# Sparse attention with one query head per period, index dots between projection slices, x reloaded by tile

## The reference

```python
rel = relu(einsum("bqhd,bsd->bqhs", iq_b, ik))      # 8 index heads of 64, one normalised index key
score = einsum("bqh,bqhs->bqs", iw_b, rel)          # weighted sum over the index heads
score = where(causal, score, -inf)
_, idx = top_k(score, 128)                          # the 128 best keys of each query
logits = q . k[idx] * 128**-0.5                     # 8 query heads of 128, 2 key/value heads
o = softmax(logits, where valid) . v[idx]
mixed = sigmoid(gate_a + ..) * o_gdn + sigmoid(gate_b + ..) * o_dsa
h = x + mixed @ w_out
```

## Time and profile before

| | us |
|---|---|
| median of 3 runs (lowest, highest) | 2372.18 (2370.74, 2373.13) |
| the profiled execution's own time | 2367.97 |
| its span, first to last instruction | 2366.2 |
| PE busy | 2260.6 |
| DVE busy | 1294.7 |
| ACT busy | 918.6 |
| POOL busy | 464.0 |

### The profile page before, as it was taken

The page is one execution under the profiler, slowest core; times in us unless marked ns, Lnnn a source line. Parts: engine busy times, 40 slices in busy tenths (PEclk is TensorE's granted clock), DMA queues, the critical chain, the costliest instruction groups (busy, mean ns, idle before and its releaser), DMA issues.

```text
span 2366.2 us, 27907 instructions
## 1 busy us (share of the span) xinstructions
PE 2260.6 (96%) x10568; PEld 1825.0 (77%) x10568; DVE 1294.7 (55%) x2044; ACT 918.6 (39%) x1626; POOL 464.0 (20%) x387
## 2 busy tenths in 40 slices
PE   5999999898899999999998999999999989999997
PEld 4887888586678888877776788888777768888885
DVE  6768333395658486765665444433566654434343
ACT  4677343226532222243454322322445553222222
POOL 0000420030111010031454210101234542101012
PEclk9999999799999999999999999999999999999998
DMA  4231312121133333222111333333221113333322
GB/s 152 89 108 62 90 45 64 53 73 44 39 106 97 98 98 97 91 89 89 54 54 36 96 97 98 98 98 96 91 86 54 41 36 98 98 98 91 98 95 83
DMA packets 68901, 194.03 MB, mean 82 GB/s; under 512 B 14496, under 2 KB 18848, under 8 KB 68768
## 3 DMA queue, kind: packets, MB, share of 16 engines
q1 hardware_dynamic: 67584, 189.89, 26.1%
q10 hardware_dynamic: 1184, 2.36, 0.3%
HBM read 185.40 MB, written 6.82 MB: 81 GB/s over the span
## 4 chain that ended last, share of the span: by engine, by line
PE 82%; DVE 5%; ACT 5%; issue 4%; POOL 2%; DMA 1%; DVEq 1%; SPq 0%; POOLq 0%; ACTq 0%
PE bank L285 17%; PE bank L287 17%; PE bank L286 17%; PE bank L321 5%; PE bank L323 5%; PE bank L322 5%; PE bank L1616 3%; PE bank L965 1%; ACT b_wh L246 1%; PE bank L1153 1%; DVE b_wl L250 1%; PE bank L1644 1%; PE bank L1643 1%; PE bank L1008 1%; PE bank L1779 1%
## 5 line engine op out<-in xcount | busy, mean ns | idle before, releaser
L246 ACT ACTIVATE b_wh<-b_raw 128x1024 fp32r<-128x1024 f32 (+1 forms) x348 | 360.1, 1035 | 1089.3 <-PE bank L287 924.9
L250 DVE TENSOR_TENSOR b_wl<-b_raw,b_wh 128x1024 fp32r<-128x1024 f32 (+1 forms) x338 | 411.5, 1217 | 132.1 <-ACT b_wh L246 131.6
L285 PE MATMUL bank<-b_xh,b_wh 128*128 128x512 f32 x1216 | 477.5, 393 | 0.4 <-DVE b_wl L250 0.4
L286 PE MATMUL bank<-b_xl,b_wh 128*128 128x512 f32 x1216 | 474.6, 390 | 0.0
L287 PE MATMUL bank<-b_xh,b_wl 128*128 128x512 f32 x1216 | 474.5, 390 | 0.0
L285 PE MATMUL bank<-b_yh,b_wh 128*128 128x512 f32 x736 | 289.8, 394 | 14.8 <-POOL b_yl L573 7.0
L287 PE MATMUL bank<-b_yh,b_wl 128*128 128x512 f32 x736 | 287.2, 390 | 0.0
L286 PE MATMUL bank<-b_yl,b_wh 128*128 128x512 f32 x736 | 287.2, 390 | 0.0
L573 POOL TENSOR_TENSOR b_yl<-b_arena,b_yh 128x512 fp32r<-128x512 f32 x66 | 111.4, 1689 | 877.7 <-ACT b_yh L551 877.7
L321 PE MATMUL bank<-b_xh,b_wh 128*128 128x512 f32 x624 | 267.9, 429 | 14.0 <-ACT b_maskSb L1941 12.9
L285 PEld LDWEIGHTS bank<-b_xh,b_wh 128*128 128x128 f32 x1216 | 229.3, 189 | 51.8 <-issue 2.5
(11 more groups left out here) (373 smaller groups left out, 2967.1 us busy)
## 6 DMA issues: line engine op xcount, KB each, us to landing
b_raw<-in_zga SPq DMA_DIRECT2D x16, 512.0 KB, 3.7
b_raw<-in_c0up SPq DMA_DIRECT2D x16, 512.0 KB, 3.6
b_raw<-in_c1up SPq DMA_DIRECT2D x16, 512.0 KB, 3.6
b_raw<-in_fqk SPq DMA_DIRECT2D x16, 512.0 KB, 3.6
b_raw<-in_s0up SPq DMA_DIRECT2D x16, 512.0 KB, 3.6
b_raw<-in_s1up SPq DMA_DIRECT2D x16, 512.0 KB, 3.6
b_raw<-in_m0up SPq DMA_DIRECT2D x16, 512.0 KB, 3.6
b_raw<-in_m1up SPq DMA_DIRECT2D x16, 512.0 KB, 3.6
```

What stands on the lines that cost most here:

```text
L246: act.activation(wh[:, par, 0:kt * P], raw[:, par, 0:kt * P], ACT.Copy).then_inc(w_hi, 1)
L250: dve.tensor_tensor(wl[:, par, 0:kt * P], raw[:, par, 0:kt * P], wh[:, par, 0:kt * P].bitcast(F32), ALU.subtract).then_inc(w_lo, 1)
L285: pe.matmul(bank[:, :], wh[:, par, w], hi[:, x, :], start=(k == 0), stop=False)
L286: pe.matmul(bank[:, :], wh[:, par, w], lo[:, x, :], start=False, stop=False)
```

## The change

- The wait for the three bf16 masks moves from the start of `conv_pe` to panel m = 12.
- Index stage: dkv, dqs and the first five gb panels (before: two) run as one sequence. The mean and the sums of the index key stand inside the first two panels. The 24 index dots stand one before each slice of panels 3 to 5. POOL makes the low halves of all 17 panels and masks each block behind its split. v is turned by PE after panel 6 and written by ACT and POOL as high and low fp32r halves.
- Attention: the units (`Attention`, `DSA`, `attn_pe` and the rest, `v_pe`, `v_copy`) are removed and replaced by the form of FoX and MLA, one query head per period (`dsa_pe`, `dsa_act`, `dsa_dve`, `dsa_pool`). Scale, mask and maximum are one DVE instruction (`tensor_tensor_reduce`) that writes to SBUF; exp works there in place. The division moves to POOL. The values are multiplied in three passes (high by high, high by low, low by high) with v as the stationary operand, so the output comes out transposed and DVE gates it straight from the bank. Three slices of gb stand in each period (`DFILL`), slices of wout's first two panels in the last one and behind it (`DTAIL`).
- x: after each tile's `yh` ACT issues the DMA of that tile of x into h; the addition to tile t waits for it alone.

```diff
+                if reloaded:
+                    dve.wait_ge(s_xt[t], 32)
...
-            pe.wait_ge(s_maskb, 3)
...
+                if m == 12:
+                    pe.wait_ge(s_maskb, 3)
...
+        DKV, DQS, GB = BASE["dkv"], BASE["dqs"], BASE["gb"]
...
+        pTd = operands("dsa_pT", arena_at + 4 * 27 * T, 2, 1280)
+        sgb = [take((12 + j) * T, T) for j in range(5)] + [take((39 + j) * T, T) for j in range(3)]
...
+        POFF = {3: 0, 2: 512, 0: 896, 1: 1024}
+        COL = {3: 0, 2: 1, 0: 2, 1: 3}
+        GROUPS = [(3,), (2, 0), (1,)]
+        TURNED = ((5, 0, 512), (6, 512, 512), (5, 1024, 256))
+        def spot(i):
+            return {3: pb[2][:, 0:512], 2: pb[3][:, 0:384], 0: pb[3][:, 384:512], 1: pb[4][:, 0:256]}[i]
+        def projected(p):
+            return DKV + p, (DS[:, 8 + p, :] if p < 4 else DS[:, p - 4, :])
...
+            def dot(u):
+                i, hh = SCORES[u]
                 rows = slice(64 * (hh % 2), 64 * (hh % 2) + 64)
                 wait(pe, i_r, u - 1)
                 pe.matmul(pb[2 + u % 2][:, 0:(i + 1) * P], DS[rows, 12 + hh // 2, B(i)], ikn[rows, 0:(i + 1) * P],
                           start=True, stop=True).then_inc(i_s, 1)
+            for p in range(12):
+                n = DKV + p
+                if p == 3:
+                    pe.wait_ge(i_kn, 1)
+                for k in range(8):
+                    if 3 <= p < 6:
+                        dot(8 * (p - 3) + k)
+                    slice_k(pe, n, n % 2, k, 8, xh, xl, 0)
+                    if p == 0 and k == 3:
+                        pe.wait_ge(out_free, DKV)
+                        pe.matmul(pb[4][:, :], M("blk64"), DS[:, 16, :], start=True, stop=True).then_inc(i_mean, 1)
+                    if p == 1 and k == 3:
+                        pe.wait_ge(i_sq, 1)
+                        norm_pe(pe, "ikn", sqk, M("blk64")[:, 0:1], row=False)
+                if p == 2:
+                    norm_pe_row(pe, "ikn")
+                if p == 6:
+                    for g in range(2):
+                        pe.wait_ge(out_free, DKV + 3 + g)
+                        for b in range(NB):
+                            m = pe.transpose(pb[5 + g][:, B(b)], DS[:, 10 + g, B(b)], ident)
+                        m.then_inc(d_vt, 1)
...
+            for p in range(12):
+                n, dst = projected(p)
+                if p == 0:
+                    act.wait_ge(i_xc, 1)
+                    act.activation(sqk, xc, ACT.Square).then_inc(i_sq, 1)
+                if 3 <= p < 6:
+                    for u in range(8 * (p - 3), 8 * (p - 3) + 8):
+                        act.wait_ge(i_s, u + 1)
+                        wait(act, i_acc, u - 1)
+                        nk = (SCORES[u][0] + 1) * P
+                        act.activation(rl[:, u % 2, 0:nk], pb[2 + u % 2][:, 0:nk], ACT.Relu).then_inc(i_r, 1)
+                split_hi(act, n + 2, (n + 2) // 2, n % 2, 8)
+                act.wait_ge(mm_done, n + 1)
+                act.activation(dst, pb[n % 2][:, :], ACT.Copy).then_inc(out_free, 1)
+                if p == 7:
+                    for g in range(2):
+                        act.wait_ge(d_vt, g + 1)
+                        act.activation(vraw[g], pb[5 + g][:, :], ACT.Copy).then_inc(d_vr, 1)
+                        act.activation(vD[:, 0, :, B(g)], blk(pb[5 + g][:, :]), ACT.Copy).then_inc(d_vh, 1)
...
-            norm_pool(pool, "ikn")
-            for i in range(1, NB):
+            def causal(i):
                 pool.wait_ge(i_acc, IDXH * i)
                 d = mask[:, i, B(i)]
                 pool.affine_select(out=d, in_=d, compare_op=ALU.is_ge, fill=FILL, base=0, pattern=[[-1, P]],
                                    channel_multiplier=1).then_inc(i_cs, 1)
+            pool.wait_ge(w_lo, DKV + 2)
+            for p in range(12 + GBF):
+                n = DKV + p
+                if p == 1:
+                    pool.wait_ge(n_ev, NROW["ikn"] + 1)
+                    pool.tensor_tensor(rowT[:, :], rowT[:, :], mhalf[:, 0:NB], ALU.pow).then_inc(n_pw, 1)
+                split_lo(pool, n + 2, (n + 2) // 2, n % 2, 8)
+                if 3 <= p < 6:
+                    causal(p - 2)
+                if p == 8:
+                    for g in range(2):
+                        pool.wait_ge(d_vr, g + 1)
+                        pool.wait_ge(d_vh, g + 1)
+                        pool.tensor_tensor(vD[:, 1, :, B(g)], blk(vraw[g]), vD[:, 0, :, B(g)].bitcast(F32), ALU.subtract)\
+                            .then_inc(d_vl, 1)
...
-                dve.tensor_scalar(sc, sc, (FILL + TAKEN) / 2, NEG, ALU.is_gt, ALU.mult).then_inc(i_mask, 1)
+            dve.drain()
...
+        GBF = 5
+        DFILL = {h_: [[(GBF + (3 * h_ + 3 + j) // 8, (3 * h_ + 3 + j) % 8)] for j in range(3)]
+                 for h_ in range(-1, 7)}
+        DFILL[7] = [[(8, 0), (8, 1)], [(8, 2), (8, 3)], [(8, 4), (8, 5)]]
+        DTAIL = [(9, 0), (9, 1), (9, 2), (9, 3), (9, 4), (9, 5), (8, 6), (9, 6), (8, 7), (9, 7)]
+        DDONE = {1: 5, 4: 6, 6: 7}
+        def dsa_pe(pe):
+            def panel_slices(some):
+                for t, k in some:
+                    n = GB + t
+                    if t < 8:
+                        slice_k(pe, n, n % 2, k, 8, xh, xl, 0)
+                    else:
+                        pe.wait_ge(y_ready, YR["gb"] + k + 1)
+                        slice_k(pe, n, n % 2, k, 8, yh, yl, 0)
+            def dots(h_):
+                for j, group in enumerate(GROUPS):
+                    wait(pe, d_m, 3 * h_ - 2 + j)
+                    for i in group:
+                        m = pe.matmul(spot(i), DS[:, h_, B(i)], DS[:, 8 + h_ // 4, 0:(i + 1) * P], start=True, stop=True)
+                    m.then_inc(d_s, 1)
+            def turn(h_, t):
+                p = dsa_p[h_ % 2]
+                if t == 0:
+                    pe.wait_ge(d_n, h_ + 1)
+                    wait(pe, d_tl, 3 * h_)
+                    for i in range(4):
+                        m = pe.transpose(pb[5][:, B(i)], p[:, POFF[i]:POFF[i] + P], ident)
+                if t == 1:
+                    for i in range(1, 4):
+                        m = pe.transpose(pb[6][:, B(i - 1)], p[:, POFF[i] + P:POFF[i] + 2 * P], ident)
+                    m = pe.transpose(pb[6][:, B(3)], p[:, POFF[3] + 3 * P:POFF[3] + 4 * P], ident)
+                if t == 2:
+                    pe.wait_ge(d_tl, 3 * h_ + 1)
+                    for i in range(2, 4):
+                        m = pe.transpose(pb[5][:, B(i - 2)], p[:, POFF[i] + 2 * P:POFF[i] + 3 * P], ident)
+                m.then_inc(d_pt, 1)
+            def values(h_, j):
+                c0, n = (0, 512, 1024, 896)[j], T - j * P
+                if j == 0:
+                    wait(pe, d_y, h_)
+                    pe.wait_ge(d_vl, 2)
+                pe.wait_ge(d_tl, 3 * h_ + (0, 1, 2, 1)[j] + 1)
+                out_, g = pb[7][:, j * P:T], h_ // 4
+                pe.matmul(out_, vD[:, 0, j, B(g)], pTd[:, 0, c0:c0 + n], start=(j == 0), stop=False)
+                pe.matmul(out_, vD[:, 0, j, B(g)], pTd[:, 1, c0:c0 + n], start=False, stop=False)
+                m = pe.matmul(out_, vD[:, 1, j, B(g)], pTd[:, 0, c0:c0 + n], start=False, stop=(j == 2))
+                if j == 2:
+                    m.then_inc(d_o, 1)
+            pe.wait_ge(out_free, DQS + 8)
+            pe.wait_ge(i_r, len(SCORES))
+            for h_ in range(-1, 8):
+                if h_ + 1 < 8:
+                    dots(h_ + 1)
+                panel_slices(DFILL[h_][0])
+                if h_ >= 0:
+                    turn(h_, 0)
+                    turn(h_, 1)
+                panel_slices(DFILL[h_][1])
+                if h_ >= 0:
+                    turn(h_, 2)
+                    for j in (0, 1, 3):
+                        values(h_, j)
+                panel_slices(DFILL[h_][2])
+                if h_ >= 0:
+                    values(h_, 2)
+            panel_slices(DTAIL)
+        def gb_gate(act, t):
+            act.wait_ge(mm_done, GB + t + 1)
+            act.activation(sgb[t], pb[(GB + t) % 2][:, :], ACT.Sigmoid, bias=V("gbb", t)).then_inc(out_free, 1)
+        def dsa_act(act):
+            for h_ in range(-1, 9):
+                if h_ + 1 < 8:
+                    p, c = dsa_p[(h_ + 1) % 2], (h_ + 1) % 2
+                    for j, group in enumerate(GROUPS):
+                        act.wait_ge(d_m, 3 * h_ + 4 + j)
+                        for i in group:
+                            nk, col_ = (i + 1) * P, slice(COL[i], COL[i] + 1)
+                            at = p[:, POFF[i]:POFF[i] + nk]
+                            m = act.activation(at, at, ACT.Exp, bias=dn[:, c, col_], scale=1.0, accum_out=ds_[:, c, col_])
+                        m.then_inc(d_e, 1)
+                if 0 <= h_ < 8:
+                    wait(act, d_o, h_)
+                    for t, (bank, c0, w) in enumerate(TURNED):
+                        act.wait_ge(d_pt, 3 * h_ + t + 1)
```

(77 more changed lines are left out.)

339 lines of the change are left out of this document (11 added, 328 removed).

## The result

| | before | after |
|---|---|---|
| median of 19 runs each (lowest to highest), us | 2370.74 (2367.49 to 2375.07) | 2375.32 (2372.5 to 2380.74) |
| profiled span, us | 2366.2 | 2371.8 |
| mean granted clock | 0.984 | 0.979 |

What follows compares the result with a forecast made beforehand. PE bounds the kernel, busy 2260.6 of 2366.2 us. Gains of 29.5 (18.6 of it the index stage) and 5.4 give 2337.3 at full clock; 10.5 for clock falls makes 2347.8, own range 2340 to 2356, with rivals 2336 to 2366.

Steps and rivals of the forecast that it cites:

- the second: Index stage, dots between slices, no idle before dkv: work besides the panels falls from 40.6 to 22.0 us, gain 18.6.
- term 4: Attention: seven gaps of PE, clock falling after three quarters of them at 2.0 us each, 10.5 us lost.
- rival D: Index panels 3 to 5: clock falls in the keys' wait, 64-row dots keep it low; 31.7 us more, 2379.5; 8%.
- The wait for the keys: Index stage: PE waits 1.8 us for the normalised keys, from DVE copy 0.69 and product 0.75, with hops.
- The mask wait: Before panel 0: PE's wait for the bf16 masks moves to m = 12, gain 4.7 to 6.1 us, taken as 5.4.
- The fused pass: Attention, DVE's scale, mask and maximum: one pass, 692 ns for 512 columns, and 0.09 us for reading the maximum out.
- rival B: Attention: the fused pass costs both passes, 1.4 us a period, and the clock falls each time: 2361 us; 15%.
- The second group's exps: Attention period: they start 5.05 us behind the start of a head's dots, ACT's copy at 6.5, period 10.7 us.
- PE's wait ahead of wout's third panel: After the attention: wout's panel 2 waits 1.8 us for ACT and DVE after panel 0's last slice.
- term 1: Start of the kernel: moving the wait for the bf16 masks gains 5.4 us, kept through the stages that follow.
- attention: One head per period of 10.7 us, set by the chain over the other engines; wout ends at 660.3 against 689.8.

Runs made afterwards that it cites:

- run 3: Kernel after with the 24 dots moved to panels 4 to 6, the wait for the keys left ahead of panel 3: 2349.01 us, ratio 0.9904.
- Run 5: Kernel after, its 3.31 us standstill kept, with each index dot over all 128 rows, which computes something else: 2336.34 us, ratio 0.9848.
- run 4: Kernel before with only the wait for the bf16 masks moved to m = 12: 2364.12 us, ratio 0.997.
- run 11: As run 1, but with the row's matmul behind the seventh slice of panel 2; PE stood 0.91 us: median 2342.23 us, ratio 0.9869.
- run 1: Kernel after with the matmul spreading the key norms moved from the end of index panel 2 to behind its third slice: 2335.7 us, ratio 0.9852.
- run 8: As run 1, with the index keys written twice, each padded with 64 zero rows, so every dot uses 128 rows: 2328.2 us, ratio 0.9814.

## Why the prediction was wrong

**The step that failed** is the second, in the sentence "The 128-row fp32 dot of 512 columns at full clock lasts 1.02 and the next starts 0.92 after it, mask product included, so 0.86 per 512 columns: 15.4 for 9216, plus 1.2 for 24 changes between kinds". It takes the dots, and the slices between them, at the full clock; term 4 counts falls of the clock in the attention only and puts this stage at none. The term was 16.6 us and measured 59.4 (75.7 for the stretch less 16.3 for its slices at full clock). Two things make up the 42.8 us:

- 8.6 us: 64-row dots are dearer than 128-row ones at the same clock. Runs 1 and 8 show 25.2 and 15.8 us for the same columns. The nearest row that was taken had another number of rows, and nothing bounded the price from above: the 28 us at 0.50 that the forecast quotes are of dots that overlap one another.
- 34.2 us: the clock. 41.5 us of dots and slices at 1.00 became 75.7 at 0.50. This is rival D, with its mechanism, place and about its price (31.7), held at 8%.

Beside them stand 1.5 us for the wait itself, 3.31 and not 1.8. That D's 2379.5 is only 4 us off the measured time is partly luck: the index stage took 13.8 us more than D has it, and the attention 12.9 less.

**Why rival D was priced too low.** Its counter-argument was that slices alone brought the clock back after 476 us. They did, and run 3 shows it again, but those slices were dense. It said nothing of a mixture in which 64-row dots hold half the time, and the one row on that, 25.34 us busy of 28 at 0.50, pointed the other way. Run 5 shows that 128 rows let the clock come back. And whether D comes true hung on the wait's length: by the times it came in 3 of 9 executions at 1.61 us, in none of 4 at 0.91 and none of 4 at 0.24, and at 3.31 all 19 timed runs of the kernel after lie at 2372.5 or above. Four executions are too few to say that 0.91 us is safe.

**The wait for the keys** was counted from DVE's 0.69 and 0.75 alone. That POOL's split of 2.3 us would begin in the middle of it followed from the new order (POOL now makes the low halves in this stage), and a DVE split beside a POOL sum was in the forecast with 2.3 instead of 1.2. The Trainium skill, "SBUF — State Buffer", Who interferes with whom, has the rule that a DVE instruction with two SBUF inputs and a POOL instruction that reads SBUF take turns at a shared port. The trace agrees, 2.45 us against 0.75. The rule was applied to the attention and not to this product, the one place where the path waited for it.

**What was right.** The mask wait: -6.2 at the end of idx, in the trace of the kernel after and in that of run 4 alike, and -7 (-4 to -10) in run 4's time, for -5.4. That is just above the term's own bounds of 4.7 to 6.1; the lower one should be 4.9, 6.1 less 1.2. The fused pass: 0.69 us for 512 columns, and the read-out 0.08 for the 0.09 taken; rival B is out. At 607.41 it ran beside POOL's division (605.12 to 607.84) and kept its 0.69; it has one SBUF input, and the same rule leaves it out, so this agrees too. The second group's exps start 4.4 us behind the dots (606.35 to 610.73) and not 5.05, and ACT's copy 1.49 us later (612.22) for 1.45, so three of the five periods read are 10.1 and not 10.7; the others are 11.7 and 10.6. That the read-out is an instruction of its own is what the Trainium skill says ("VectorE: DVE Perf Modes", Two Vector instructions with no wait between them), and the trace agrees. PE's wait ahead of wout's third panel was 1.79 for 1.8. In the kernel after PE never waited for the mask.

**Term 4, the falls in the attention,** was too dear here: one fall in place of five, though PE stood 2.6 to 3.2 us at seven turns. Windows of the kernel after behind two such waits:

```profile
592.00:595.00 3.00, 3.00 (x11) 2.71 (x11) 1.36 (x3) 2.49 (x4) 3.00 (x3) 0.50 0.34 90
...
603.50:606.00 2.50, 2.50 (x14) 2.24 (x15) 0.99 (x2) 0.90 (x2) 2.42 (x2) 1.00 0.35 101
```

It doesn't look like a constant of the kernel: the attention is the same in run 11, and its clock fell more often. Four gaps of the kernel before were too few to give a share.

**The balance.** -0.8 (term 1), +45.5 (index stage: 42.8, 1.5 for the wait, 1.2 left), -12.9 (attention: 2.4 faster than laid out and no 10.5 for the clock) make the 31.8 us by which wout ended late against the forecast; 1.8 came back later. The gain that was forecast is there, and more: without the low clock in the dots it is 35 us (run 1), and with 128 rows as well 44 us (run 8).

## What to carry to other kernels

Before heavy work is put between instructions that are known to run at the low clock, ask what the low clock will then cover: here it took in 16 us of slices, which became 31, and took the dots apart, which became 45 in place of 26. Look for the wait just ahead of such a stretch and close it with work that is already there; here one matmul moved by five slices was worth 40 us. Try padding a contraction of 64 rows to 128 with zeros where an engine off the path can write them: here it gave another 7.5 us.

## What the hardware showed

- A 64-row fp32 dot of 512 columns between 128-row slices takes 1.26 us at clock 1.00, a 128-row one 0.88 (steps of 1.94 and 1.56 less 0.68). Runs 1 and 8 give the same over all sizes: 25.2 and 15.8 us for 24.
- At clock 0.50 a 64-row fp32 dot of 512 columns takes 2.30 us between 128-row slices (kernel after) and 1.38 next to other 64-row dots (kernel before).
- With PE busy for 75.7 of 75.7 us the clock stayed at 0.50, as long as 64-row dots stood between the slices. The same mixture with no wait ahead of it stayed at 1.00 for 41.5 us (run 1). With 128 rows and the wait the clock was back within 5 us (run 5).
- The same kernel with the same wait of 1.61 us took either way from one execution to the next, 2338 to 2342 or 2371 to 2377 us.
